# Second block of a two-block model: mix product, double norms, query product, feed-forward input split and final store taken tile by tile

## The reference

```python
def rmsnorm(x, gain):
    x32 = x.astype(jnp.float32)
    y = x32 * lax.rsqrt(jnp.mean(x32 * x32, axis=-1, keepdims=True) + RMS_EPS)
    return (y * gain.astype(jnp.float32)).astype(x.dtype)

def memory_cross_attention(xn, memn, wq, wk, wv, wo):
    q = (xn @ wq).reshape(b, s, CROSS_HEADS, CROSS_HEAD_DIM)
    ...                                     # k, v from the memory; 4 heads of 128
    p = jax.nn.softmax(logits, axis=-1)
    o = jnp.einsum('bhsm,bmhd->bshd', p, v)...
    return o @ wo

def conv_glu_ffn(xn, w_up, conv_w, conv_b, w_down):
    gate, up = jnp.split(xn @ w_up, 2, axis=-1)              # 1024 -> 2 x 2816
    gate = causal_dwconv(gate, conv_w) + conv_b
    return (jax.nn.silu(gate) * up) @ w_down

def second_block(x, mem, ...):
    h = token_mixer(rmsnorm(x, norm_mix_pre), ..., w_mix_out)   # ends in y @ w_out, 1024 x 1024
    x = x + rmsnorm(h, norm_mix_post)
    h = memory_cross_attention(rmsnorm(x, norm_cross_pre), rmsnorm(mem, mem_norm), ...)
    x = x + rmsnorm(h, norm_cross_post)
    h = conv_glu_ffn(rmsnorm(x, norm_ffn_pre), ...)
    return x + rmsnorm(h, norm_ffn_post)
```

## Time and profile before

| | us |
|---|---|
| median of 3 runs | 1614.17 |
| range of the runs | 1611.98 to 1616.63 |
| the profiled execution's own time | 1617.86 |
| its span, first to last instruction | 1615.9 |
| mix product to the end of the store, of that span | 1287.9 to 1615.9 |

### The profile page before, as it was taken

One profiled execution on the slowest core, in us unless ns is written; L12 is line 12 of the kernel. 1 busy time (PEld: TensorE's weight loads), 2 busy tenths in 40 slices (PEclk: granted clock), 3 DMA queues, 4 the chain that ended last, 5 costly groups with the idle time before them and its releaser, 6 DMA issues.

```text
span 1615.9 us, 17742 instructions
## 1 busy us (share of the span) xinstructions
PE 1398.9 (87%) x6756; PEld 897.4 (56%) x6756; DVE 680.1 (42%) x1210; ACT 396.8 (25%) x628; POOL 107.4 (7%) x42
## 2 busy tenths in 40 slices
PE   5998876688978999999999999499878767599996
PEld 2444366677544444444444445377656436299985
DVE  3044566255463222222222222564365532467763
ACT  0121322321011222222212212245221011335442
POOL 0013224640000000000000000000000000000000
PEclk8998857769878999999999999599659887699998
DMA  8772112531461999999999995654601121145552
GB/s 306 234 235 65 48 70 78 183 104 53 156 270 60 402 421 412 421 409 420 415 415 417 419 408 209 233 160 131 130 0 53 53 104 52 52 157 183 183 185 76
DMA packets 95583, 338.68 MB, mean 210 GB/s; under 512 B 10072, under 2 KB 36345, under 8 KB 66730
## 3 DMA queue, kind: packets, MB, share of 16 engines
q1 hardware_dynamic: 84162, 319.08, 51.7%
q10 hardware_dynamic: 11113, 18.37, 4.1%
q0 software_dynamic: 256, 0.52, 0.1%
HBM read 332.94 MB, written 1.05 MB: 207 GB/s over the span
## 4 chain that ended last, share of the span: by engine, by line
PE 77%; DVE 13%; DMA 3%; ACT 3%; issue 2%; POOL 1%; ACTq 1%; DVEq 0%; POOLq 0%
PE bank L1665 14%; PE bank L1269 10%; PE bank L1681 7%; PE bank L1284 6%; PE bank L1286 5%; PE bank L1285 5%; PE bank L1296 2%; PE bank L1628 2%; PE bank L1629 2%; PE bank L1646 2%; PE bank L1648 2%; PE bank L1776 2%; POOL ring L2036 1%; DMA ada_ring<-in_ada_w 1%; PE bank L1486 1%
## 5 line engine op out<-in xcount | busy, mean ns | idle before, releaser
L1269 PE MATMUL bank<-ring,xT 128*128 128x512 f32 (+3 forms) x480 | 199.3, 573 | 6.6 <-DVE xT L2072 3.3
L1269 PEld LDWEIGHTS bank<-ring,xT 128*128 128x128 f32 x480 | 95.7, 217 | 100.7 <-issue 91.1
L1681 PE MATMUL bank<-dn,tmp 128*64 128x512 f32 x528 | 120.6, 598 | 0.0
L2595 DVE TENSOR_TENSOR xT<-bank,mod 128x512 fp32r<-128x512 f32 x66 | 45.6, 691 | 158.0 <-ACT mod L1043 150.7
L2588 DVE SCALAR_TENSOR_TENSOR tmp<-silu_c,rc,bank 128x256 f32<-128x256 f32 x33 | 22.6, 684 | 196.8 <-ACT silu_c L1030 191.4
L1284 PE MATMUL bank<-mod,w_high 128*128 128x256 f32 x352 | 100.0, 284 | 5.3 <-DVE xT L2973 5.3
L1286 PE MATMUL bank<-mod,ring 128*128 128x256 f32 x352 | 99.4, 283 | 0.0
L1285 PE MATMUL bank<-xT,w_high 128*128 128x256 f32 x352 | 98.3, 279 | 0.0
L2962 DVE TENSOR_TENSOR ring<-ring,w_high 128x1024 fp32r<-128x1024 f32 x66 | 77.6, 1220 | 21.9 <-ACT w_high L1211 20.3
L1296 PE MATMUL bank<-c_ident,xn 128*128 128x128 f32 x120 | 28.2, 415 | 63.8 <-DVEq L2658 25.4
L2036 POOL TENSOR_TENSOR ring<-ring 128x2048 f32<-128x2048 f32 x16 | 72.6, 4536 | 78.7 <-ACT ring L936 78.0
(11 more groups left out here) (582 smaller groups left out, 2583.3 us busy)
## 6 DMA issues: line engine op xcount, KB each, us to landing
dn<-in_exp_w_down SPq DMA_DIRECT2D x66, 1024.0 KB, 10.6
ring<-in_exp_w_gate SPq DMA_DIRECT2D x34, 1024.0 KB, 9.6
ring<-in_exp_w_up SPq DMA_DIRECT2D x34, 1024.0 KB, 11.7
gu_odd<-in_exp_w_gate SPq DMA_DIRECT2D x32, 1024.0 KB, 10.2
gu_odd<-in_exp_w_up SPq DMA_DIRECT2D x32, 1024.0 KB, 12.2
ring<-in_w_ffn_in SPq DMA_DIRECT2D x22, 1024.0 KB, 5.1
ring<-in_ada_w SPq DMA_DIRECT2D x16, 1024.0 KB, 4.9
ring<-in_w_in SPq DMA_DIRECT2D x7, 2048.0 KB, 10.4
```

The source lines that it names most:

```text
L1269: mm = pe.matmul(bank[lin_bank(o)][:, 0:n], lhs(k, t), ring[:, j % RING, k * n:(k + 1) * n], start=(k == 0), stop=(k == kt - 1 and not bias))
L1681: mm = pe.matmul(bank[6 + h][CHUNKS[c], :], act_eT[:, 0, k, CHUNKS[c]], dn[:, 2 * parity + c, lo:lo + BANK], start=(k == 0), stop=(k == D_ ...
```

## The change

Work of the second block that was done for both tiles at each step is done for one tile and then for the other:

- The mix product is computed tile by tile (both jobs for tile 0, then both for tile 1). The last output is cut in two halves of four k, and the transposes of tile 0's `xn` stand between them.
- Both double norms run for tile 0 from start to end, then for tile 1. VectorE sums the squares of `x` for both tiles; ScalarE no longer helps there.
- The query product runs as 64 matmuls of 128 columns instead of 32 of 256: all heads for tile 0, the transposes of tile 1, all heads for tile 1.
- Before the feed-forward part the high and low parts of `xT` are made per tile and per four k, between the other steps of VectorE; TensorE's first product waits for the low part of four k at a time. `split_low(0)` is cut in its two pieces. In `in2` the low part is made in two halves.
- At the end each tile is squared, normed, added and stored by itself (two stores of 0.5 MB).

Since output numbers follow the order of computation, `w_cq` is now issued when the third output of the mix product is done (job 0, tile 1).

```diff
+if kind == "mix":
+    if jobs[j - 1][0] != "mix":
+        for t in range(T):
+            for half in range(2):
+                outputs[(j + half, t)] = len(outputs)
+    continue
...
-sp.wait_ge(out_ready, 1)
-sp.dma_start(out.rearrange("(t p) d -> p t d", p=P), x[:, :, :]).then_inc(store_done, 16)
-sp.wait_ge(store_done, 16)
+for t in range(T):
+    sp.wait_ge(out_ready, t + 1)
+    sp.dma_start(out[t * P:(t + 1) * P, :], x[:, t, :]).then_inc(store_done, 16)
+sp.wait_ge(store_done, 16 * T)
...
+def tile_square(src, t):
+    act.activation(xn[:, t, :], src[:, t, :], ACT.Square, accum_out=small[:, 16 + t:17 + t])\
+        .then_inc(sq_done, 1)
+def tile_rstd(t):
+    rstd(small[:, 18 + t:19 + t], small[:, 16 + t:17 + t])
 for j in range(2):
-    for t in range(T):
-        lin_copy(J_MIX + j, t, hbuf[:, t, j * BANK:(j + 1) * BANK])
+    lin_copy(J_MIX + j, 0, hbuf[:, 0, j * BANK:(j + 1) * BANK])
+act.wait_ge(lin_evac, after(J_MIX + 1, 0))
+tile_square(hbuf, 0)
+tile_rstd(0)
+lin_copy(J_MIX, 1, hbuf[:, 1, 0:BANK])
+tile_rstd(0)
+lin_copy(J_MIX + 1, 1, hbuf[:, 1, BANK:2 * BANK])
 act.wait_ge(lin_evac, after(J_MIX + 1, 1))
-squares([hbuf[:, t, :] for t in range(T)], [xn[:, t, :] for t in range(T)], wait=False)
-rstd(small[:, 18:20], small[:, 16:18])
-squares([x[:, 1, :]], [xn[:, 1, :]])
-rstd(small[:, 18:20], small[:, 16:18])
+tile_square(hbuf, 1)
+tile_rstd(1)
+tile_rstd(1)
...
-for i in range(4):
-    act.wait_ge(lin_mm, after(J_CO, i))
-    act.activation(hbuf[:, i // 2, (i % 2) * BANK:(i % 2 + 1) * BANK],
-                   bank[outputs[(J_CO, i)] % 2][:, :], ACT.Copy).then_inc(lin_evac, 1)
-act.wait_ge(lin_evac, after(J_CO, 3))
-squares([hbuf[:, t, :] for t in range(T)], [xn[:, t, :] for t in range(T)], wait=False)
-rstd(small[:, 18:20], small[:, 16:18])
-squares([x[:, 1, :]], [xn[:, 1, :]])
-rstd(small[:, 18:20], small[:, 16:18])
-act.wait_ge(h_used, 3)
+for t in range(T):
+    for i in range(2 * t, 2 * t + 2):
+        act.wait_ge(lin_mm, after(J_CO, i))
+        act.activation(hbuf[:, t, (i % 2) * BANK:(i % 2 + 1) * BANK],
+                       bank[outputs[(J_CO, i)] % 2][:, :], ACT.Copy).then_inc(lin_evac, 1)
+    act.wait_ge(lin_evac, after(J_CO, 2 * t + 1))
+    if t == 0:
+        tile_square(hbuf, 0)
+        tile_rstd(0)
+tile_rstd(0)
+tile_square(hbuf, 1)
+tile_rstd(1)
+def x_high(t):
+    for g in range(2):
+        act.wait_ge(tp_evac, TP_FF + 2 * t + g + 1)
+        c = (slice(None), slice(4 * g, 4 * g + 4), slice(t * P, (t + 1) * P))
+        act.activation(xT_high[c], xT[c], ACT.Copy).then_inc(x_high_made, 1)
+x_high(0)
+tile_rstd(1)
+act.wait_ge(h_used, 2)
...
+x_high(1)
 split_high(1)
+act.wait_ge(h_used, 3)
...
-act.wait_ge(x2_ready, 3)
-squares([hbuf_f[:, t, :] for t in range(T)], [xT[:, 4 * t:4 * t + 4, :].rearrange("p k c -> p (k c)") for t in range(T)], wait=False)
-rstd(small[:, 18:20], small[:, 16:18])
+    act.wait_ge(x2_ready, 2 + t)
+    act.activation(xT[:, 4 * t:4 * t + 4, :].rearrange("p k c -> p (k c)"), hbuf_f[:, t, :], ACT.Square,
+                   accum_out=small[:, 16 + t:17 + t]).then_inc(sq_done, 1)
+    tile_rstd(t)
...
-pe.wait_ge(x_low_made, 1)
 for u in range(2 * N_IN2):
+    if u < 2:
+        pe.wait_ge(x_low_made, u + 1)
...
-for j in range(2):
-    dense(J_MIX + j, xTk)
-transpose_all(xn, layer=5)
-pe.wait_ge(tp_evac, TP_XN + 4)
-for i in range(2):
-    for quarter in range(4):
-        dense_T_quarter(J_CQ, i, quarter)
+dense_tile(J_MIX, 0, xTk)
+dense_tile(J_MIX + 1, 0, xTk)
+dense_tile(J_MIX, 1, xTk)
+dense_tile(J_MIX + 1, 1, xTk, part=(0, 2))
+transpose_all(xn, layer=5, tiles=(0,))
+dense_tile(J_MIX + 1, 1, xTk, part=(1, 2))
+def queries(t):
+    pe.wait_ge(tp_evac, TP_XN + 2 * t + 2)
+    for i in range(2):
+        o = outputs[(J_CQ, i)]
+        if t == 0:
+            if i == 0:
+                full[J_CQ % RING] += 16 * len(jobs[J_CQ][4])
+                pe.wait_ge(w_full[J_CQ % RING], full[J_CQ % RING])
+            pe.wait_ge(lin_evac, o - 1)
+        for h in range(2):
+            lo = (2 * h + t) * P
+            for k in range(KT):
+                w = k * CW + (2 * i + h) * CHD
+                mm = pe.matmul(bank[o % 2][:, lo:lo + P], ring[:, J_CQ % RING, w:w + CHD], xTk(k, t),
+                               start=(k == 0), stop=(k == KT - 1))
+        if t:
+            mm.then_inc(lin_mm, 1)
+queries(0)
+transpose_all(xn, layer=5, tiles=(1,))
+queries(1)
...
-pe.wait_ge(tp_evac, TP_FF + 4)
-pe.wait_ge(x_low_made, 2)
...
+                if u == half == 0 and k % 4 == 0:
+                    pe.wait_ge(x_low_made, 2 + 3 + k // 4)
...
-dve.tensor_tensor(xT_low[:, :, :], xT[:, :, :], xT_high.bitcast(F32), ALU.subtract).then_inc(x_low_made, 1)
+for i in range(2):
+    k = slice(4 * i, 4 * i + 4)
+    dve.tensor_tensor(xT_low[:, k, :], xT[:, k, :], xT_high[:, k, :].bitcast(F32), ALU.subtract)\
+        .then_inc(x_low_made, 1)
...
-dve.wait_ge(lin_evac, after(J_MIX + 1, 1))
-add_normed(hbuf, MIX_POST)
-dve.sem_inc(h_used, 1)
+def tile_add_normed(src, t, g):
+    asked[0] += 1
+    dve.wait_ge(sq_done, asked[0])
+    rsqrt_mean(small[:, 16 + t:17 + t], small[:, 16 + t:17 + t], D, RMS_EPS)
+    link(dve.scalar_tensor_tensor(src[:, t, :], src[:, t, :], small[:, 18 + t:19 + t], gain_of(g),
+                                  ALU.mult, ALU.mult))
+    link(dve.tensor_tensor(x[:, t, :], x[:, t, :], src[:, t, :], ALU.add))
+def tile_norm(t, g):
+    sum_squares(small[:, 16 + t:17 + t], x[:, t, :])
+    rsqrt_mean(small[:, 16 + t:17 + t], small[:, 16 + t:17 + t], D, RMS_EPS)
+    link(dve.scalar_tensor_tensor(xn[:, t, :], x[:, t, :], small[:, 18 + t:19 + t], gain_of(g),
+                                  ALU.mult, ALU.mult))
+    dve.sem_inc(xn_ready, 1)
 dve.wait_ge(late_gains, 16 * N_LATE)
-norm_into(xn, x, CROSS_PRE, ready=xn_ready)
-untranspose()
+for t in range(T):
+    tile_add_normed(hbuf, t, MIX_POST)
+    if t:
+        dve.sem_inc(h_used, 1)
+    tile_norm(t, CROSS_PRE)
+    untranspose(tiles=(t,))
...
-dve.wait_ge(lin_evac, after(J_CO, 3))
-add_normed(hbuf, CROSS_POST)
-dve.sem_inc(h_used, 1)
-norm_into(xn, x, FFN_PRE, ready=xn_ready)
-for i in range(2):
-    link(dve.memset(gateT[:, i, :, 0:2], 0.0))
-dve.sem_inc(h_used, 1)
-untranspose()
+for t in range(T):
+    tile_add_normed(hbuf, t, CROSS_POST)
+    if t:
+        dve.sem_inc(h_used, 1)
+    tile_norm(t, FFN_PRE)
+    if t == 0:
+        untranspose(tiles=(0,))
...
+def x_low(t, g):
+    dve.wait_ge(x_high_made, 1 + 2 * t + g + 1)
+    c = (slice(None), slice(4 * g, 4 * g + 4), slice(t * P, (t + 1) * P))
+    dve.tensor_tensor(xT_low[c], xT[c], xT_high[c].bitcast(F32), ALU.subtract).then_inc(x_low_made, 1)
+x_low(0, 0)
+x_low(0, 1)
+split_low(0, (0,))
+untranspose(tiles=(1,))
+x_low(1, 0)
+x_low(1, 1)
+split_low(0, (1,))
+for i in range(2):
+    link(dve.memset(gateT[:, i, :, 0:2], 0.0))
+dve.sem_inc(h_used, 1)
 split_low(1)
...
-dve.wait_ge(x2_ready, 3)
-add_normed(hbuf_f, FFN_POST)
-dve.sem_inc(out_ready, 1)
+for t in range(T):
+    tile_add_normed(hbuf_f, t, FFN_POST)
+    dve.sem_inc(out_ready, 1)
```

More of the change, by code:

```diff
@@ L1219, in _ @@
             split_high(0)
-            act.wait_ge(tp_evac, TP_FF + 4)
-            act.activation(xT_high, xT[:, :, :], ACT.Copy).then_inc(x_high_made, 1)
+            x_high(1)
             split_high(1)
+            act.wait_ge(h_used, 3)
             for i in range(FF_JOBS):
@@ L1305, in score_bank, with transpose_all @@
                 return bank[6 + n % 2]
-            def transpose_all(src, kt=KT, layer=None):
-                for t in range(T):
+            def transpose_all(src, kt=KT, layer=None, tiles=range(T)):
+                for t in tiles:
                     if layer:
@@ L2072, in tp_copy, with untranspose @@
                 dve.tensor_copy(dst, src.rearrange("p (i c) -> p i c", i=split)).then_inc(tp_evac, 1)
-            def untranspose(kt=KT):
-                for t in range(T):
+            def untranspose(kt=KT, tiles=range(T)):
+                for t in tiles:
                     for g in range(kt // 4):
@@ L2658, in norm_into @@
                         dve.sem_inc(ready, 1)
-            def add_normed(src, g):
-                norm_into(src, src, g, by_act=2)
-                for t in range(T):
-                    link(dve.tensor_tensor(x[:, t, :], x[:, t, :], src[:, t, :], ALU.add))
             dve.wait_ge(first_gains, 32)
@@ L2955, in ffn_act, with split_low @@
                     .then_inc(act_ready, 1)
-            def split_low(u):
-                for q in range(PIECES):
+            def split_low(u, pieces=range(PIECES)):
+                for q in pieces:
                     dve.wait_ge(high_made, u * PIECES + q + 1)
@@ L2969, in act_split_low @@
                     .then_inc(act_low_made, 1)
-            split_low(0)
-            dve.wait_ge(x_high_made, 2)
-            dve.tensor_tensor(xT_low[:, :, :], xT[:, :, :], xT_high.bitcast(F32), ALU.subtract).then_inc(x_low_made, 1)
+            def x_low(t, g):
```

(1 more changed line is left out.)

## The result

The changed kernel takes 1587.62 us in the median of 4 runs (1582.76 to 1590.74), the kernel before beside it 1613.08 (1610.86 to 1616.63): ratio 0.9837, 95% interval 0.9803 to 0.9872, 21 to 32 us. The profiled execution took 1589.89 us, its span is 1588.1 (before 1617.86 and 1615.9).

What follows compares the result with a forecast made beforehand. Outside the TensorE-bound feed-forward part, VectorE and ScalarE taking turns at the norms bound the gaps. Terms 12.7 + 6.4 + 4.3 - 0.1 = 23.3 us off 1614.17 gave 1591 us; own range 1588 to 1594, whole 1587 to 1599.

Steps and rivals of the forecast that it cites:

- Gap 1: Mix product to query product: tile-by-tile norm and queries end at 1334.3 instead of 1347.02, gain 12.7 us.
- rival (c): Query product: weight loads not hidden at 128 columns, 0.22 us a record, 13.5 us later, 1604.5 us; chance 4%.
- Rival (a): Query product: TensorE's clock falls between the halves, costing 2.4 us, at most 7.1; time 1593.5 to 1598; chance 20%.
- The cross attention keeps its instructions and is only earlier: Cross attention, 28.00 us: same instructions, only earlier; no gain of its own predicted (0).
- Gap 2: Output product to first feed-forward product: it starts at 1407.9 instead of 1414.34, gain 6.4 us.
- the upper bound: Output product to feed-forward: gain up to 7.4 us if tile 0's transposes run at the full clock.
- Rival (b): Before feed-forward: wait not shortened, VectorE the bound, price up to 6.4 us, time 1597.5; chance 10%.
- The end: Final norm and store: 3.1 us from the norm, 1.2 from the half-size store; gain 4.3 us, bounds 3.1 to 5.1.
- in2: Low part made in halves there gains nothing; one more instruction costs about 0.1 us.
- Rival (d): Feed-forward part: TensorE's clock falls inside it, slower than before, over 1619 us from 56 us at half clock; chance 3%.
- The sum: Whole kernel: 12.7 + 6.4 + 4.3 - 0.1 = 23.3 us gained, from median 1614.17 to 1591 us.
- the whole range: Whole kernel's time: 1587 to 1599 us, against the forecast's own range of 1588 to 1594.

Runs made afterwards that it cites:

- e6: Kernel before with only the query product's form changed to 64 matmuls of 128 columns, behind all transposes; 1613.46 against 1616.34 us, ratio 0.9989.
- e1: Kernel before with only mix product, first double norm and query product taken tile by tile; 1599.19 against 1614.42 us, ratio 0.9908.
- e5: Changed kernel with the query product back at 256 columns behind tile 1's transposes; 1601.3 against 1616.34 us for the kernel before, ratio 0.9911.
- e9: Kernel before with three extra unread 128-column matmuls ahead of the 256-column query product; one run, 1610.35 us beside a median of 1616.07.
- e7: Changed kernel with tile 1's scale/add earlier, its second square sum on ScalarE, root table preloaded; 1586.0 against 1616.34 us (kernel before), ratio 0.9806.
- e2: Kernel before with only the second double norm and feed-forward high and low parts tile by tile; 1607.4 against 1614.42 us, ratio 0.9945.
- e4: Kernel before with only the low part of xT in front of in2 made in two halves; 1614.15 against 1614.42 us, ratio 0.9989.

## Why the prediction was nearly right, and which step failed

**Gap 1**: forecast 12.7, measured 12.5 us (with the mix product's -0.9). The steps came where they were put, counted from the last mix copy: first norm step of tile 1 after 1.81 us (forecast 1.88), second half of the queries after 10.49 (10.6), last query copy after 17.94 (17.7). The weights were in place 0.6 us after that copy (forecast 0.4), so TensorE waited 0.6 us for them; behind the first half it waited 0.5 us again, for tile 1's norm, so that the later issue cost nothing in the end. 64 records took 7.4 us, not 7.1. The rival (c) falls: a record takes 0.116 us, not 0.22, the loads are busy 7.22 us beside the matmuls' 7.38, and e6 shows it without the change. For float32 matmuls of 128 columns the rule on row groups of the Trainium skill ("TensorE: Matmul & The Clock Gate", section "Part 3: Packing small matmuls — row/col tiling") does not agree with the records here: their loads are hidden, though all of them use all rows. The same section of the Trainium skill also lets a load go ahead when it targets the background weight buffer; no trace here shows which of the array's buffers a load targets. Rival (a) falls too: the clock is 1.00 over the whole gap.

**The cross attention keeps its instructions and is only earlier**: this step failed. The instructions are the same and it is earlier, but its duration is not a property of its instructions. The second line of the earlier trace rows showed 0.66 there, and the prediction did not use it. For the clock between the queries' halves it read the 0.60 of gap 1 and the 0.53 of the output product and priced a fall, but it did not ask what the new order does to the clock behind gap 1, and put that at nothing without a reason. Before, the upper level lasted 5.4 us into the cross attention; now it lasts 10.7 us. The old gap 1 gives 27.98 to 28.04 us in four executions, the new one 25.99 to 26.14 in three, e1 with gap 1 alone among them, and e5 with the wait back 27.8. Term: 0 forecast, 1.9 us measured; it is most of what separates the forecast from the result.

How far it is a gain of the change itself is less than e1 alone suggests. e9 reached 23.5 us with the old order, its long wait, and three extra matmuls of 0.7 us. So short waits in gap 1 are not what the value hangs on; the change happened to bring the clock to a pattern worth 1.9 us, three matmuls in the old kernel to one worth 4.5. Why the one is better than the other stays open.

**Gap 2**: forecast 6.4, measured 6.76, less 0.2 in the output product. VectorE was the bound, as the prediction's order has it, and e7 shows this from the other side: one sum of squares taken off its path and two steps reordered gave 2.6 us. e2 shows the upper bound, 7.5 us, with tile 0's transposes at the full clock. Rival (b) falls.

**The end**: forecast 4.3, measured 4.4. The guess on the half-sized store, 1.2 us less than 4.0, was near: it landed after 2.6.

**in2**: forecast -0.1; e4 tells nothing from zero. Rival (d) falls: the feed-forward part is 184.36 us against 184.29.

**The sum**: 23.3 forecast, 25.3 measured from the mix product on, of which 1.9 are the cross attention. The medians differ by 25.5. The time stayed inside the whole range by 0.6 us only: that range was widened downwards for gap 2's upper bound, which did not come about in the changed kernel, and it was the cross attention, for which nothing had been allowed, that used the room.

## What to carry to other kernels

Where TensorE waits for a chain of short steps, taking the work tile by tile hides part of the product in the chain, and here the shorter waits also kept the clock up through that gap. What the new order does to the clock behind the gap is another matter, and has to be measured: it gave 1.9 us here, and three extra matmuls in the old order gave 4.5. So a stretch whose granted clock is below 1 has no fixed duration: whenever an edit moves a wait ahead of it, the range should take in what the stretch would need at the full clock (here 22.3 us against 28.0 at 0.66). And what is saved ahead of a product that starts at the low level can be lost again in its first microseconds (1.2 of 2.6 us in e7). Before reordering anything, try the cheap thing: extra matmuls in the waits, on operands that lie ready, gave 8 us more in the profile here, and 6 to 7 in a part that the change leaves alone.
